# Splitting the modulation slabs of the first layer around its Fourier transform

## The reference

```
sh1, sc1, g1, sh2, sc2, g2 = split(silu(c) @ ada_w[0] + ada_b[0], 6)   # for c and for c_ctx
h   = rmsnorm(x, norm_g[0, 0]) * (1 + sc1) + sh1                        # the same for ctx
x   = x + g1 * (real(fft2(h grouped by 256 columns)) @ fnet_wo + fnet_bo)
h   = rmsnorm(x, norm_g[0, 1]) * (1 + sc2) + sh2
x   = x + g2 * expert_choice_moe(h)                                     # 16 experts
```

## Time and profile before

| | us |
|---|---|
| median of 3 runs | 3818.35 |
| lowest and highest | 3816.11, 3818.69 |
| the profiled execution, its time | 3827.83 |
| its span on the core | 3826.0 |

### The profile page before, as it was taken

How to read it: one execution, slowest core, us unless ns; L and a number is a source line. 1 busy time by engine, 2 the same in 40 slices (tenths; PEclk the granted TensorE clock), 3 DMA queues, 4 the chain that set the end, 5 groups by cost and what they waited for, 6 DMA issues and landing times.

```text
span 3826.0 us, 84150 instructions
## 1 busy us (share of the span) xinstructions
PE 3626.3 (95%) x35394; PEld 2267.6 (59%) x35394; DVE 1574.6 (41%) x3428; ACT 802.6 (21%) x1807; POOL 730.7 (19%) x644
## 2 busy tenths in 40 slices
PE   5999999999989898899999999999999999999998
PEld 4544444455557777764344344455888744558887
DVE  1421111164466666653122133742545437425454
ACT  1210010020145555541000011061000010610000
POOL 3200000000034434420000000002343300023433
PEclk8999999999999999999999999999999999999999
DMA  9399999942300000012999981101222211012221
GB/s 378 126 397 375 376 391 362 392 203 78 116 11 13 14 18 17 14 54 112 424 428 429 428 361 45 66 24 44 89 88 88 97 45 66 24 44 89 88 89 44
DMA packets 56483, 626.44 MB, mean 164 GB/s; under 512 B 5920, under 2 KB 9248, under 8 KB 20640
## 3 DMA queue, kind: packets, MB, share of 16 engines
q1 hardware_dynamic: 49808, 599.68, 39.2%
q0 software_dynamic: 3968, 14.16, 1.3%
q10 hardware_dynamic: 2448, 8.91, 0.6%
HBM read 604.64 MB, written 18.09 MB: 163 GB/s over the span
## 4 chain that ended last, share of the span: by engine, by line
PE 84%; DVE 6%; DMA 3%; issue 3%; ACT 2%; DVEq 1%; ACTq 1%; SPq 0%
PE bank L987 68%; PE bank L1540 11%; DMA work<-slabs 3%; PE bank L1922 1%; PE bank L1935 1%; PE bank L1595 1%; DVE hx L2721 1%; PE bank L1015 1%; DMA ring<-slabs 1%; DVE work L2697 1%; ACTq L2601 0%; ACT work L2600 0%; DVE work L2706 0%; DVE work L3121 0%; PE bank L1403 0%
## 5 line engine op out<-in xcount | busy, mean ns | idle before, releaser
L987 PE MATMUL bank<-work 128*64 128x512 f32 (+10 forms) x5142 | 855.2, 426 | 14.6 <-issue 5.2
L987 PEld LDWEIGHTS bank<-work 128*64 128x64 f32 (+5 forms) x5142 | 493.5, 153 | 347.3 <-issue 267.6
L987 PE MATMUL bank<-ring,work 128*64 128x512 f32 (+4 forms) x4506 | 498.4, 436 | 53.2 <-DMA ring<-slabs 44.6
L987 PE MATMUL bank<-hx,ring 128*128 128x512 f32 (+1 forms) x1344 | 483.8, 516 | 5.1 <-DVE hx L2721 2.8
L987 PE MATMUL bank<-work,ring 128*128 128x256 f32 (+1 forms) x1616 | 481.3, 457 | 6.6 <-DVE work L3062 3.4
L987 PEld LDWEIGHTS bank<-work,ring 128*128 128x128 f32 x1616 | 307.5, 191 | 173.9 <-issue 133.3
L987 PEld LDWEIGHTS bank<-ring,work 128*32 128x32 f32 (+3 forms) x4506 | 210.7, 126 | 326.0 <-issue 272.2
L987 PEld LDWEIGHTS bank<-hx,ring 128*128 128x128 f32 x1344 | 256.2, 192 | 220.5 <-issue 200.4
L3757 POOL TENSOR_TENSOR work<-ring 128x512 f32<-128x512 f32 (+1 forms) x44 | 69.3, 1576 | 1565.5 <-ACT work L2148 1167.8
L2697 DVE TENSOR_TENSOR work<-work,bank 128x256 f32<-128x256 f32 x240 | 91.9, 416 | 384.3 <-ACT work L2675 380.8
L1540 PE MATMUL bank<-work 64*64 64x64 f32 x9216 | 193.3, 225 | 32.3 <-issue 20.4
(11 more groups left out here) (390 smaller groups left out, 4547.7 us busy)
## 6 DMA issues: line engine op xcount, KB each, us to landing
ring<-slabs SPq DMA_DIRECT2D x177, 2048.0 KB, 10.8
work<-slabs SPq DMA_DIRECT2D x82, 2048.0 KB, 15.5
hx<-slabs SPq DMA_DIRECT2D x17, 2048.0 KB, 10.0
work<-kv SPq DMA_DIRECT2D x18, 384.0 KB, 3.1
kv<-work SPq DMA_DIRECT2D x2, 3072.0 KB, 15.6
kv<-work ACTq DMA_DIRECT2D x6, 512.0 KB, 6.3
resx<-xT SPq DMA_DIRECT2D x1, 2048.0 KB, 11.4
kv<-work POOLq DMA_DIRECT2D x1, 2048.0 KB, 29.5
```

The source lines that it names most:

```text
L987: return pe.matmul(out, lhsT, rhs, start=(k == 0), stop=(k == n - 1))
```

## The change

The front is put in another order, and its work is spread over other engines.

- **Slabs.** The list becomes a0 to a5, w0, w1, a6 to a9, tables, a10, a11: a are the modulation slabs, w the two slabs of `fnet_wo`, tables the slab of the transform. The waves C and S are loaded by a small transfer of their own (514 columns) behind the context. SyncE loads slab n + 3 when slab n is used; for w0 and w1 it waits for GpSimd's sums. The three slabs behind the list are loaded when tables, a10 and a11 are used.
- **Sums of squares.** ScalarE squares x only, VectorE the context; VectorE adds tiles in pairs, so that TensorE sums 4 tiles of each, ahead of slab a0.
- **Fold.** VectorE scales and folds x, GpSimd the context. GpSimd sums w0 and w1 after VectorE's fold.
- **Modulation.** It is copied, turned and applied in three groups of four slabs. The transform over channels needs group 0 only. TensorE's order is: sums, a0 to a3, turn, first half of the transform, a4, a5, second half, a6, a7, turn, a8, a9, sequence stage, a10, a11, router shift, turn, output product.
- **Router.** The widened router (L2772) is made after group 2, no longer ahead of the transform.
- **Fill.** The 12 unread products ahead of the gather become 4.

```diff
...
+FRONT = ["a0", "a1", "a2", "a3", "a4", "a5", "w0", "w1", "a6", "a7", "a8", "a9", "tables", "a10", "a11"]
...
-            sp.dma_start(resx[:, :, :], x_d.rearrange("(k p) t -> p k t", p=128)).then_inc(tables_loaded, 16)
-            sp.dma_start(resc[:, :, :], ctx_d.rearrange("(k p) t -> p k t", p=128)).then_inc(tables_loaded, 16)
+            sp.dma_start(resx[:, :, :], x_d.rearrange("(k p) t -> p k t", p=128)).then_inc(x_loaded, 16)
+            sp.dma_start(resc[:, :, :], ctx_d.rearrange("(k p) t -> p k t", p=128)).then_inc(context_loaded, 16)
+            sp.dma_start(waves, slabs_d[FRONT.index("tables")][:, 0:FN["S"][1]]).then_inc(waves_loaded, 16)
...
-            single(0, ADA_SLABS, 0)
             f0 = ADA_SLABS + FNET_SLABS
+            used = 0
+            for n in range(f0 - RING):
+                if FRONT[n] in ("w0", "w1"):
+                    sp.wait_ge(norm_pool, 2 + int(FRONT[n][1]))
+                else:
+                    used += 1
+                    sp.wait_ge(slab_used, used)
+                load(n + RING)
...
+            sp.wait_ge(norm_pool, 4)
+            for n in range(f0 - RING, f0):
+                used += 1
+                sp.wait_ge(slab_used, used)
+                load(n + RING)
...
+                q = n % 4
                 for k in range(KT):
                     for g in range(4):
-                        m = mm(P[n][32 * g:32 * g + 32, 0:128], cs[:, k, :], w[:, k, 128 * g:128 * g + 128], k, KT)
-                m.then_inc(filled, me.add("filled"))
+                        m = mm(P[7][32 * g:32 * g + 32, 128 * q:128 * q + 128], cs[:, k, :], w[:, k, 128 * g:128 * g + 128], k, KT)
+                if q == 3:
+                    m.then_inc(ad_pe, ad.one("summed", n // 4))
                 pe.drain().then_inc(slab_used, 1)
+
+            def ada_turned(g):
+
+                pe.wait_ge(*ad_done("act", "copied", g))
+                if g:
+                    pe.wait_ge(*ad_done("dve", "mod", g - 1))
+                for q in range(4):
+                    m = pe.transpose(P[6][:, 128 * q:128 * q + 128], adarow[:, (4 * g + q) * 128:(4 * g + q + 1) * 128], ident)
+                m.then_inc(ad_pe, ad.one("turned", g))
...
+            pe.wait_ge(*ad_done("dve", "context"))
+            for k in range(4):
+                mm(P[5][:, 0:NC], ones, sqc0[:, k, :], k, 4)
+            for k in range(4):
+                pe.wait_ge(*ad_done("dve", "added", k))
+                m = mm(P[4][:, :], ones, sqx0[:, k, :], k, 4)
+            m.then_inc(ad_pe, ad.one("sums"))
...
+            for n in range(4):
                 ada_slab(n)
-            for k in range(KT):
-                square_sum(k, [(sqx0, P[6], NX), (sqc0, P[7], NC)])
-            me.t["na"].n += 1 + KT
...
+            ada_turned(0)
...
+                for n in (4, 5) if pair == 0 else ():
+                    ada_slab(n)
+            me.t["slab"].n += 2
+            ada_slab(6)
+            ada_slab(7)
             pe.wait_ge(fed, me.next("fed"))
+            ada_turned(1)
+            ada_slab(8)
+            ada_slab(9)
+            pe.wait_ge(slab_loaded[me.slot()], me.landed())
+            tables = flat(me.next_slab())
...
+            pe.drain().then_inc(slab_used, 1)
+            ada_slab(10)
+            ada_slab(11)
...
+            ada_turned(2)
...
-                kept_warm(P[1], 12)
+                kept_warm(P[1], 4)
...
-            tile_squares([(resx, sqx0), (resc, sqc0)], wait=False)
-            root(rstd, [(P[6], NX), (P[7], NC)])
...
+                act.wait_ge(*ad_done("pe", "summed", g))
+                act.activation(adarow[:, 512 * g:512 * g + 512], P[7][:, :], ACT.Copy).then_inc(ad_act, ad.one("copied", g))
...
+            act.wait_ge(x_loaded, 16)
+            for k in range(4):
+                for half in range(2):
+                    tile_square(k + 4 * half, [(resx, sqx0)], wait=False)
+            act.wait_ge(*ad_done("pe", "sums"))
...
+            ada_copied(0)
+            act.wait_ge(*ad_done("dve", "mod", 0))
...
+            ada_copied(1)
+            act.wait_ge(asked, me.next("asked"))
...
+            ada_copied(2)
...
+            v.wait_ge(context_loaded, 16)
+            tt(sqc0, resc[:, :, :], resc[:, :, :], ALU.mult)
+            v.drain()
+            v.tensor_tensor(sqc0[:, 0:4, :], sqc0[:, 0:4, :], sqc0[:, 4:8, :], ALU.add).then_inc(ad_dve, ad.one("context"))
+            for k in range(4):
+                v.wait_ge(norm_act, 2 * k + 2)
+                v.tensor_tensor(sqx0[:, k, :], sqx0[:, k, :], sqx0[:, k + 4, :], ALU.add).then_inc(ad_dve, ad.one("added", k))
+            v.wait_ge(norm_act, KT + 1)
+            tt(ux, resx[:, :, :], bc(rstd[:, 0:NX].unsqueeze(1), 128, KT, NX), ALU.mult)
+            v.drain()
+            half = NX // 2
+            near, far = ux[:, :, 1:half], ux[:, :, NX - 1:half:-1]
+            tt(hx[:, :, 1:half], near, far, ALU.add)
+            tt(hx[:, :, half + 1:NX], near, far, ALU.subtract)
+            tt(hx[:, :, 0:1], ux[:, :, 0:1], ux[:, :, 0:1], ALU.add)
+            v.tensor_tensor(nyq[:, :, 0:1], ux[:, :, half:half + 1], ux[:, :, half:half + 1], ALU.add).then_inc(ad_dve, ad.one("folded"))
...
+            modulation(0)
+            gained(0)
...
+            v.tensor_scalar(ghalf, mod[:, 0, 1, :, :], 0.5, None, ALU.mult).then_inc(ad_dve, ad.one("mod", 0))
+            v.drain()
+            v.wait_ge(norm_pool, 1)
...
-            for j in range(2):
-                m = v.tensor_tensor(wide_router[:, j, :, 0:NE], router[:, 0, :, :], bc(mod[:, 0, 4, :, j:j + 1], 128, KT, NE), ALU.mult)
-            m.then_inc(rt_dve, rt.one("router"))
...
+            modulation(1)
...
+            modulation(2)
...
+            for j in range(2):
+                m = v.tensor_tensor(wide_router[:, j, :, 0:NE], router[:, 0, :, :], bc(mod[:, 0, 4, :, j:j + 1], 128, KT, NE), ALU.mult)
+            m.then_inc(rt_dve, rt.one("router"))
...
-            for res, u, n, at in ((resx, ux, NX, 0), (resc, uc, NC, NX)):
-                pool.tensor_tensor(u, res[:, :, :], rstd[:, at:at + n].unsqueeze(1).to_broadcast([128, KT, n]), ALU.mult)
+            pool.tensor_tensor(uc, resc[:, :, :], rstd[:, NX:NX + NC].unsqueeze(1).to_broadcast([128, KT, NC]), ALU.mult)
...
-            for u, h, n, j in ((ux, hx, NX, 0), (uc, hc, NC, 1)):
...
-            pool.wait_ge(norm_dve, KT)
+            pool.wait_ge(*ad_done("dve", "folded"))
...
-                pool.tensor_tensor(wsum[1][:, 4 * half:4 * half + 4, :], w[:, 0:4, :], w[:, 4:8, :], ALU.subtract).then_inc(norm_pool, 1)
+                pool.tensor_tensor(wsum[1][:, 4 * half:4 * half + 4, :], w[:, 0:4, :], w[:, 4:8, :], ALU.subtract)
+                pool.drain().then_inc(norm_pool, 1)
+            me.t["slab"].n = FRONT.index("tables")
+            pool.wait_ge(slab_loaded[me.slot()], me.landed())
+            pool.tensor_copy(w128[0:4, :], flat(me.next_slab())[0:4, FN["w128"][0]:FN["w128"][1]]).then_inc(norm_pool, 1)
```

More of the change, by code:

```diff
@@ L292 @@
 XS_BANK = {"xs0": 2, "xs1": 3, "xsc0": 0, "xsc1": 1}
+AD_PE = [("sums",)] + [(_n, _g) for _g in range(3) for _n in ("summed", "turned")]
+AD_DVE = [("context",)] + [("added", _k) for _k in range(4)] + [("folded",)] + [("mod", _g) for _g in range(3)]
+AD_ACT = [("copied", _g) for _g in range(3)]
+FRONT = ["a0", "a1", "a2", "a3", "a4", "a5", "w0", "w1", "a6", "a7", "a8", "a9", "tables", "a10", "a11"]
 RT_PE = [(_n,) for _n in ("shift", "spread", "raw", "root", "logits", "gates", "index", "tables")]
-RT_DVE = [(_n,) for _n in ("router", "shift", "spread", "rows", "less", "soft", "best", "index", "tables")]
+RT_DVE = [(_n,) for _n in ("shift", "router", "spread", "rows", "less", "soft", "best", "index", "tables")]
 RT_ACT = [(_n,) for _n in ("root", "exp")]
@@ L491, in build @@
         gate_bias = cut(work, WORK - 2 * KT, KT, 2)
-        adarow = work[:, 0:ADA_SLABS * 128]
+        waves = work[:, 0:FN["S"][1]]
+        adarow = work[:, 1024:1024 + ADA_SLABS * 128]
         cs = cut(work, WORK - 2 * KT - KT * 32, KT, 32)
@@ L1058, in dense_summed @@
                 kept_warm(P[1], 1 if n > 2 else 2)
-            pe.wait_ge(tables_loaded, 64)
-            pe.wait_ge(answered, 1)
-            pe.wait_ge(fed, me.next("fed"))
+            ad = Steps(AD_PE)
+            pe.wait_ge(tables_loaded, 32)
             def ada_slab(n):
@@ L1093, in late_rows_turned @@
                 m.then_inc(late_turned, 1)
-            for n in range(RING):
-                ada_slab(n)
-            for k in range(KT):
-                square_sum(k, [(sqx0, P[6], NX), (sqc0, P[7], NC)])
-            me.t["na"].n += 1 + KT
[L1100 to L1119, removed]
+            pe.wait_ge(*ad_done("dve", "context"))
[5 more added lines that the diff above has]
+            m.then_inc(ad_pe, ad.one("sums"))
+            me.t["na"].n += 1 + 2 * KT
+            me.t["nd"].n += KT
+            pe.wait_ge(answered, 1)
+            pe.wait_ge(fed, me.next("fed"))
+            for n in range(4):
```

(27 more changed lines are left out.)

62 lines of the change are left out of this document (34 added, 28 removed).

## The result

The changed kernel takes 3830.31 us, the kernel before 3817.76 us (medians of 7 runs each). The ratio is 1.0032, with a 95% interval of 1.0021 to 1.0043: it is slower by 12.5 us where 6.6 us less were forecast, and it lies outside the range of 3804 to 3821. The profiled execution of the changed kernel took 3828.49 us (span 3826.7), an ordinary one. That of before took 3827.83, 10 us above the median of its own runs, so the ends of the two profiles must not be compared; the front can be.

A forecast was written before the change was run, and what follows sets the result against it. TensorE, busy 95% of the span, was taken as the bound, so changes count only where it waits. Front 2.9 plus routing 3.7 gives 6.6 us off 3818.35, forecasting 3811.8 us; 8-in-10 range 3804 to 3821.

The forecast's parts named there:

- Root: Front, after the sums of squares: root ready at 28.8 us, 19.9 us earlier.
- fold: Front, after the root: VectorE's and GpSimd's folds take turns, so their times add, ending at 48.0 us.
- start of the transform: Front, after the fold: first transform product at 49.9 us, against 89.5 before.
- slab chain: Front, w1 through GpSimd's sums to a8, a9 and tables: tables land at 99.9, sequence stage starts at 100.0, was 108.40.
- overlapping folds: Rival in the front: both engines' folds run beside each other, transform starts 5.2 us earlier, 3806.6 us; chance 0.18.
- 1.0 more for half a clock level at its start (between nothing and 2): Sequence stage: 1.0 us added to its 16.6 us, since a8 and a9 arrive with waits.
- given back to TensorE's clock: Rival: half clock at sequence start and first experts (2 + 2), two issue stalls (4); 3817 us, chance 0.26.
- The forecast's last line: Sign: sequence stage starting before 96 or after 104, or experts under 4 us earlier than 229.44, makes the prediction wrong.
- 3.7 us gained: Routing, at the gather: shorter fill starts the turn 4.2 us earlier, less 0.5 for half clock; bounds 2 and 4.2.
- slower rival: Rival in the slab chain: a9 and tables take 9.0 us each instead of 4.9; 3820 us, chance 0.14.
- first part: The front up to the output product: starts at 122.8 against 125.68, a gain of 2.9 us.

The follow-up runs named there:

- run 8: Run 4's kernel with GpSimd's scaling and fold of the context held until VectorE's fold of x is done: 3811.54 us.
- run 5: The kernel before with five VectorE clears ahead of the signal that opens the sequence stage, so TensorE idles there: 3847.09 us, ratio 1.0068.
- run 6: The changed kernel with 5 unread 512-column products inside the sequence stage, behind its first two banks, and none ahead of it: 3821.86 us.
- Run 10: The changed kernel with run 2's fill ahead of the sequence stage and no unread products ahead of the gather: 3816.23 us.
- run 4: The changed kernel with the edits of run 2 and run 3 together: 3812.40 us, ratio to before 0.9981.
- run 2: The changed kernel with 5, 2 and 3 unread products in the waits ahead of a8, a9 and the tables slab: 3815.43 us, ratio to before 0.9987.
- run 3: The changed kernel with 12 unread products ahead of the gather instead of 4: 3831.86 us; its profiled execution took 3817.04 us.
- run 7: The changed kernel with only 3 unread products between a9 and the tables wait, and 12 ahead of the gather: 3820.19 us.
- run 9: Run 4's kernel with 11 more unread products ahead of the column sums and 4 ahead of the transform: 3814.43 us.

## Why the prediction was wrong

- *Root, fold, start of the transform, slab chain: right.* Root forecast 28.8, measured 28.8; fold 48.0, measured 46.3; transform 49.9 and 48.1; tables 99.9 and 96.4. Of the 3.5 us at the end the fold gave 1.7, and the steps behind it were each some tenths of a us to 1 us shorter than forecast. The overlapping folds fall (run 8).
- *"1.0 more for half a clock level at its start (between nothing and 2)": this step failed.* The stage took 29.1 us against 16.6 + 1.0, so the term measured 12.5, and a10 behind it took another 1.7 (3.64 us at half for 1.95). With the 3.5 us gained ahead, the output product came 9.7 us later than forecast (132.5 for 122.8). The course was wrong too: the term took the stage to begin at half clock and to rise within some us; it was at full clock for its first 2 us and at half for the other 27, and did not rise. I had read from the first slabs and from the transform that TensorE's clock comes back within some us of work, and applied it to a stage whose own products don't bring it back (runs 5, 6). The rows of before showed that stage at full clock from end to end and said nothing of the other case. I had bounded the unknown by the nearest case instead of by both levels over the whole stage, which by the slabs' 3.64 for 1.95 us would have given 0 to 14 us.
- *The rival "given back to TensorE's clock" named the cause and had its size wrong*: 2 us for this stage. With 12.5 in its place its sum is 7 to 12 us slower than before. The forecast's last line asked for experts that start at least 4 us before 229.44; they started at 235.19.
- *Routing, "3.7 us gained": failed too, as size.* Between output product and first expert the changed kernel saved 1.1 us in the profile (102.7 for 103.8). The timed runs put 4 products 2.0 us above 12 (-0.1 to 4.0) and none 3.8 above. The release of the gather came from 6.9 to 10.7 us after the fill's start over the twelve profiles that have such a fill, by nothing that I varied. With 12 products TensorE came to the turn 1.2 to 6.6 us after the release, and that is what a shorter fill can save; it pays with the turn (up to 0.9 us more). The clock of the first experts is no sure price: they took 16.13 to 19.00 us in the eight profiles with 12 products and 17.69 to 18.69 in the three with 4. The Trainium skill advises against idle time between bursts of products (TensorE: Matmul & The Clock Gate, why this matters). Run 10 agrees, with TensorE idle for 7.72 us ahead of the turn and the kernel 3.8 us slower than with 12 products; for 4 products against 12 the runs don't settle it. The row that I set against the advice was one sample of the gather.
- *The slower rival* (one transfer under way for a9 and tables) fell: a9 and tables landed 4.9 us apart.
- *Sum.* With the stage at full clock and 12 products, the reordered front is worth 7.4 us (run 4), where its first part was forecast at 2.9. The missing clock costs 15.4 us (run 2 against the changed kernel), the short fill about 2, which is not clear of nothing.
- *Open.* At the start of the experts the changed kernel is 5.8 to 6.7 us behind the two profiles of before, in the medians 12.5. The rest arises later, where nothing is changed, or lies in the spread of single executions; I haven't settled it. Open too is which property of the stage's products (2 rows in some, 127 to 257 columns, a new weight tile for each) keeps the clock from rising, and what makes the clock fall within the stage. In the two profiled executions that lost it TensorE had been idle at full clock for 1.2 us just ahead of the stage, in those that kept it for 0.6 at most (before, and run 3). No run varies this idle time alone.

## What to carry to other kernels

When a stage is moved behind waits, price it at both levels of the clock over its whole length: a stage at 100% busy need not win its clock back, and a full clock at its entry can still be lost. Read the clock around the entry in windows of 1 us; in one of 4 us the 2 us at full clock show only as 0.80. Unread full-width products in the waits ahead of such a stage saved more than they took here (runs 2, 6, 7), and nothing that the timed runs could show further ahead, where the fold and transfers set the pace (run 9). A split of `tensor_tensor` operations with two inputs in SBUF between VectorE and GpSimd took about as long as the sum of both (17.5 us for 9.0 and 9.2, run 8).

## What the runs showed of the hardware

- TensorE, without a gap and at 100% busy, stayed at half clock for 30.8 us (run 5) and at full clock for 16.6 us in the same 74 instructions. The two differ in the idle time ahead, 9.28 us and 0.60, and so in the level at entry.
- A full clock at entry didn't hold by itself: the stage lost it after 2.1 us in the changed kernel and after 2.4 us in run 6. Under products of 128 rows and 512 columns it came back 1.1 us after they began (run 6).
- VectorE's `tensor_scalar` of 16 elements with one input in SBUF took 2.16 us beside a GpSimd fold (run 8), 0.17 us in the changed kernel, where no fold was running. So it is not only operations with two SBUF inputs that wait. The Trainium skill (SBUF — State Buffer, who interferes with whom) lists `tensor_scalar` among those that can contend, in a mode that uses two ports; no trace here shows the mode.
- The indirect gather for the first experts was released 6.9 us (run 7) to 10.7 us (the changed kernel) after the start of the fill, the same point of the program.
